# Moving modulation pieces between the stages of a weight stream, and a weight split ahead of the attention's quotients

## What is computed

```python
for l in range(DEPTH_2):
    mod = jax.nn.silu(c) @ w_ada[l] + b_ada[l]
    sh1, sc1, g1, sh2, sc2, g2 = jnp.split(mod[:, None, :], 6, axis=-1)
    h = x * (1.0 + sc1) + sh1
    y = token_mixer(h, ...)
    x = layer_norm_2(DEEPNORM_ALPHA * x + g1 * y, ln1_g[l], ln1_b[l])
    h = x * (1.0 + sc2) + sh2
    y = conv_ffn(h, ...)
    x = layer_norm_2(DEEPNORM_ALPHA * x + g2 * y, ln2_g[l], ln2_b[l])
```

## Time and profile before

| | |
|---|---|
| median of 3 runs | 1767.1 us |
| the profiled execution | 1769.27 us, span 1767.5 us |
| PE busy | 1724.4 us (98%) |
| DVE busy | 1488.2 us (84%) |
| ACT busy | 1101.6 us (62%) |
| POOL busy | 288.7 us (16%) |
| low halves on DVE | 469, 577.9 us |
| ada pieces on DVE | 96, 116.7 us |
| chain that ended last | PE 69%, DVE 15%, ACT 8% |

### The profile page before, as it was taken

How to read it: one execution, slowest core, us unless ns; L and a number is a source line. 1 busy time by engine, 2 the same in 40 slices (tenths; PEclk the granted TensorE clock), 3 DMA queues, 4 the chain that set the end, 5 groups by cost and what they waited for, 6 DMA issues and landing times.

```text
span 1767.5 us, 28648 instructions
## 1 busy us (share of the span) xinstructions
PE 1724.4 (98%) x10356; PEld 1508.1 (85%) x10356; DVE 1488.2 (84%) x2896; ACT 1101.6 (62%) x2180; POOL 288.7 (16%) x396
## 2 busy tenths in 40 slices
PE   9999999999999999999998999999999899999997
PEld 8888888888888888888887888888888888988886
DVE  6999879877799999699986888788787788789887
ACT  6888665554575555688863555576665456566664
POOL 3995000000000000298700000012000300002000
PEclk9999999999999999999998999999999999999999
DMA  7446658845558988344554744546764654546662
GB/s 246 149 150 191 194 179 287 264 164 189 199 195 289 318 293 298 122 148 137 188 177 155 238 144 144 197 126 203 225 197 150 212 196 129 174 140 190 224 184 80
DMA packets 92733, 339.48 MB, mean 192 GB/s; under 512 B 10288, under 2 KB 10672, under 8 KB 91952
## 3 DMA queue, kind: packets, MB, share of 16 engines
q1 hardware_dynamic: 92592, 337.64, 58.8%
HBM read 336.55 MB, written 1.05 MB: 191 GB/s over the span
## 4 chain that ended last, share of the span: by engine, by line
PE 69%; DVE 15%; ACT 8%; issue 4%; POOL 2%; DMA 1%; SPq 0%; ACTq 0%; DVEq 0%; POOLq 0%
PE ps L104 68%; DVE wl L120 6%; ACT tmp L110 3%; ACT wh L113 3%; POOL B L120 2%; PE ps L107 2%; DVE B L120 1%; DVE raw L130 1%; DVE tmp L130 1%; DVE tmp L120 1%; DMA cb<-in_cb 1%; DVE sm L142 1%; ACT B L110 1%; DVE sc L151 1%; ACT os L113 1%
## 5 line engine op out<-in xcount | busy, mean ns | idle before, releaser
L104 PE MATMUL ps<-XS,wh 128*128 128x256 f32 (+2 forms) x3152 | 782.0, 330 | 24.2 <-DVE wl L120 17.3
L120 DVE TENSOR_TENSOR wl<-raw,wh 128x1024 fp32r<-128x1024 f32 x469 | 577.9, 1246 | 93.6 <-ACT wh L113 91.5
L104 PEld LDWEIGHTS ps<-XS,wh 128*128 128x128 f32 (+1 forms) x3152 | 527.9, 193 | 81.0 <-issue 28.6
L104 PE MATMUL ps<-XS,wl 128*128 128x256 f32 x2136 | 581.3, 283 | 0.0
L113 ACT CAST wh<-raw 128x1024 fp32r<-128x1024 f32 x469 | 477.2, 1045 | 101.6 <-PE ps L104 94.6
L104 PEld LDWEIGHTS ps<-XS,wl 128*128 128x128 f32 x2136 | 409.6, 192 | 11.4
L120 POOL TENSOR_TENSOR B<-B,tmp 128x236 f32<-128x236 f32 (+11 forms) x368 | 244.2, 705 | 628.6 <-ACT tmp L110 612.7
L104 PE MATMUL ps<-wh,os 128*128 128x512 f32 x864 | 280.3, 392 | 0.9 <-DVE wl L120 0.5
L104 PE MATMUL ps<-B,raw 128*128 128x256 f32 x1024 | 226.1, 380 | 0.0
L130 DVE SCALAR_TENSOR_TENSOR ps<-B,C,ps 128x253 f32<-128x253 f32 (+17 forms) x560 | 216.7, 477 | 2.8 <-ACT ps L110 2.8
L104 PEld LDWEIGHTS ps<-B,raw 128*128 128x128 f32 x1024 | 192.6, 190 | 28.4 <-issue 2.9
(11 more groups left out here) (172 smaller groups left out, 1667.3 us busy)
## 6 DMA issues: line engine op xcount, KB each, us to landing
raw<-in_w SPq DMA_DIRECT2D x628, 512.0 KB, 4.4
B<-in_ln SPq DMA_DIRECT2D x4, 1024.0 KB, 6.0
C<-in_cst SPq DMA_DIRECT2D x1, 1103.5 KB, 9.2
X<-in_x SPq DMA_DIRECT2D x2, 512.0 KB, 4.6
out_x<-X SPq DMA_DIRECT2D x4, 256.0 KB, 2.5
cb<-in_cb SPq DMA_DIRECT2D x1, 512.0 KB, 13.7
pos<-in_pos SPq DMA_DIRECT2D x1, 160.0 KB, 5.5
raw<-in_w SPq DMA_DIRECT2D x1, 128.0 KB, 3.9
```

Of the source, the lines that this page charges most:

```text
L104: return NOTHING if self.e is None else self.e.matmul(*a, **k)
L120: return NOTHING if self.e is None else self.e.tensor_tensor(o, a, b, op)
```

## The change

The ada pieces keep their number and their order among themselves. The plan puts them elsewhere: 2 in a0 (after `o10` and `o11`), 45 in b, 26 in c, 1 in a1 (after `o10`), 7 in m0, 8 in f0 and 7 in m1. Among the heads there are now 26 instead of 12: one after each `b.z` from 2 on and one after each of `b.o2` to `b.o13`. In the token mixers none is left among `iq` and `qk`; three stand at `cq0`, `cq1` and `ckv` and four at the gate units `g8`, `g10`, `g12` and `g14`. In `dve_b`, `feed_dve("b.z{h}")` now stands ahead of `dve_quotients`. Two parts of the rotary work move: the first steps go ahead of a1's `z7`, and the spreading goes to m0, behind `feed_dve("m0.wr", 2)`.

```diff
-def plan_a(j):
+def plan_a(j, u):
...
     for k in range(16):
         out.append((f"{A}.o{k}", [("a_w_out", j, 128 * k, 128, 0, D)], "split"))
+        if k in ((10,) if j else (10, 11)):
+            out.append(ada_piece(j, next(u)))
     return out
...
@@ plan_b
-            if h > 1 and h % 2 or h in (4, 6, 10, 12, 14):
+            if h > 1:
                 out.append(ada_piece(0, next(u)))
         if h >= 2:
             out.append((f"b.o{h - 2}", [("b_w_out", 0, 128 * (h - 2), 128, 0, D)], "split"))
+            if 4 <= h < 16:
+                out.append(ada_piece(0, next(u)))
...
@@ plan_c
-            if i and (i < 14 or kind in "cu"):
+            if i and kind in "cu":
                 ada()
...
@@ plan_m
     for n in range(4):
         one(f"iq{n}", tiles(w, l, O_IQ + 128 * n))
-        if n < (3 if l else 4):
-            ada()
     for n in range(2):
         one(f"cq{n}", tiles(w, l, O_CQ + 128 * n))
+        ada()
     one("ckv", tiles(w, l, O_CKV))
+    ada()
     for n in range(8):
         one(f"qk{n}", tiles(w, l, 128 * n))
-        ada()
...
             one(f"g{n}", tiles(w, l, (O_GB if n < 8 else O_GA) + 128 * (n % 8)))
+            if n in (8, 10, 12, 14):
+                ada()
...
@@ plan_f
-            a = next(u, None) if i >= 18 else None
+            a = next(u, None) if 8 <= i < 16 else None
...
@@ dve_a
         self.feed_dve(dve, f"{A}.z6.1", 0)
+        if j:
+            self.dve_rope_turns(dve)
         self.feed_dve(dve, f"{A}.z7.0", 0)
...
             if j and i == 16:
                 self.dve_rope(dve)
-            if j and i == 18:
-                self.dve_rope_spread(dve)
...
@@ dve_b
+            h = st - 1
+            if 0 <= h < 16:
+                self.feed_dve(dve, f"b.z{h}")
             if st < 16:
                 self.dve_quotients(dve, self.tmp[st % 3], self.stat(st), ("b", st))
             if st == 1:
                 turned(10)
-            h = st - 1
-            if 0 <= h < 16:
-                self.feed_dve(dve, f"b.z{h}")
...
@@ dve_m
         self.feed_dve(dve, f"{M}.wr", 2)
+        if l == 0:
+            self.dve_rope_spread(dve)
```

More of the change, by code:

```diff
@@ L220, in plan_a, with plan_b @@
         out.append((f"{A}.o{k}", [("a_w_out", j, 128 * k, 128, 0, D)], "split"))
+        if k in ((10,) if j else (10, 11)):
+            out.append(ada_piece(j, next(u)))
     return out
-def plan_b():
+def plan_b(u):
     out = []
-    u = iter(range(48))
     def chunk(which, n, base, adas, kps=range(4)):
@@ L251, in plan_b @@
             out.append((f"b.o{h - 2}", [("b_w_out", 0, 128 * (h - 2), 128, 0, D)], "split"))
-    return out, u
+            if 4 <= h < 16:
+                out.append(ada_piece(0, next(u)))
+    return out
 def plan_c(u, u1):
@@ L370, in plan @@
 def plan():
-    b, u = plan_b()
-    u1 = iter(range(48))
-    out = plan_a(0) + b + plan_c(u, u1) + plan_a(1)
+    u, u1 = iter(range(48)), iter(range(48))
+    out = plan_a(0, u) + plan_b(u) + plan_c(u, u1) + plan_a(1, u1)
     u = u1
@@ L1358, in rope_views, with dve_rope_turns @@
         return [self.m["G"][64:96, k * T:k * T + T] for k in range(4)]
-    def dve_rope(self, dve):
+    def dve_rope_turns(self, dve):
         s, m, r = self.s, self.m, slice(64, 96)
@@ L1376, in dve_rope, with step @@
         dve.ts(k, k, -MAGIC, None, ALU.add, None).then_inc(s["rope"].up(3), 1)
+    def dve_rope(self, dve):
+        s = self.s
+        a, k, w, pf = self.rope_views()
+        def step(n):
+            dve.wait_ge(*s["rope"][n])
         step(3)
```

## The result

| | before | after |
|---|---|---|
| median of 10 runs | 1767.05 us | 1773.28 us |
| lowest to highest | 1765.9 to 1769.23 us | 1769.69 to 1774.7 us |
| profiled execution | 1769.27 us, span 1767.5 | 1769.69 us, span 1767.9 |

The ratio is 1.0032, 95% interval 1.0022 to 1.0042: slower by 6 us, where 16 were forecast. The two profiled executions differ by 0.4 us alone. Before's lies just above its ten runs, after's is the shortest of its ten; the other nine took 1772.2 to 1774.7 us, at a mean granted clock of 0.995 or 0.996 where the profiled one had 0.998. So I read the profile after as the change without the clock term; the first experiment tests that.

The account below looks back on a forecast made before the run. PE was taken as the bound, short of work in the mixing layers and hardly in the heads. Stage terms summed to +2.4 us, the clock added +13.2: 1767.1 + 15.6 = 1783 us, range 1765 to 1795.

Parts of the forecast that it names:

- the clock term: Heads and a0: half-speed stretches behind eleven new PE waits, taken at 1.2 us each, +13.2 us.
- Heads: Ten rounds of heads: a loop through DVE, PE and ACT makes each round 10.10 us, PE waiting 2.5: +22.9 us.
- Rival 3: Heads: the loop doesn't close, as o{st-3}'s cast is done before head st's maxima end; 1752 us, chance 0.08.
- a0, a1, m0's entry, f0: Stages outside heads and mixing layers: a0 +3.1, a1 +0.2, m0's entry -1.0, f0 +1.5 us.
- m0 and m1: Mixing layers: PE's waits behind ada pieces mostly go and the clock recovers; m0 -9.9, m1 -14.4 us.
- The mean clock over the ten rounds: Heads, a sign of the forecast: mean granted clock near 0.85, half of 3.35 us lost in each 11.3.
- Rival 2: Heads: PE waits 2.5 us a head but the clock holds its upper level; 1769.5 us, chance 0.18.

Follow-up runs that it names:

- the first experiment: The changed kernel once more, without an edit, to profile another execution: 1775.87 us.
- the longer waits above: The changed kernel with a useless DVE maximum ahead of the low halves of o3 to o12: 1797.05 us with 1024 columns, 1781.66 us with 256.

## Why the prediction was too high

- **Heads.** Right in mechanism and size: 10.08 us a round against 10.10, a wait of 2.24 to 2.5. The stage lost 25.5 instead of 22.9, as the first of the waits is 3.5 us, the low half of `b.z5` is late by 0.6 as well, and another 0.9 comes behind the tenth round. Rival 3 is excluded by the rows: the cast stands behind the exponentials.
- **a0, a1, m0's entry, f0.** 3.6 against 3.1, 0.1 to 0.4 against 0.2, -1.0 against -1.0, 1.6 against 1.5.
- **m0 and m1.** Too small a gain: -13.2 against -9.9 and -16.1 against -14.4. Two things were left out. DVE's backlog from the ada pieces had reached as far as the gate units `g0` and `g1`, where PE waited too (about 1 us a unit in either layer, gone now). And the half-speed stretch at m0's entry, which was to stay, is gone (1.4 us), though the wait ahead of it is 1.4 us still. In the kernel before it stands here:

```profile
940.90:944.10 3.20, 3.20 (x16) 3.20 (x16) 1.64 (x4) 1.71 (x6) 0.00 (x0) 0.50 0.00 0
```

- **The clock in the heads and a0: the step that failed.** It took 1.2 us for each of eleven waits, 13.2; in the median run the term is about 3.6 by my estimate, which is what that run has beyond the profiled execution. A stretch costs more than that where it comes (1.5, and 2.7 where it is double), but it doesn't come behind each: none of eleven in one profile, three in another. The mean clock over the ten rounds, forecast near 0.85, was 1.00 in the one and 0.95 in the other. Without the clock term the sum is +2.4. The two profiled executions, of which the second has no such stretch, differ by +0.4; the median after lies 3.6 above its profiled execution, and the median before 2.2 below, which makes the 6.2. That +2.4 came so near to +0.4 is in part luck: b and a0 lost 3.1 more than forecast, and m0 and m1 gave 5.0 more. The reason that was given, that the waits of the mixing layers were of this size and had 0.50 beside them, took length for the cause; the longer waits above show that it isn't by itself.
- **Rival 2** came nearest: 1769.5 with the clock held. It was given 0.18, and the row that spoke for it (1.00 throughout the heads) was discounted, since its waits were short. The median lies between it and the forecast, nearer to it.

By the section "HAM oscillation — how this bites in real kernels" of the Trainium skill's "TensorE: Matmul & The Clock Gate", which warns only of longer idle gaps than a0's and nine of the ten in the heads, that rival would have been the forecast. The runs agree with it in part: in the profile after no wait had 0.50 behind it, the first of 3.5 us included, and in the next profile eight of the ten in the heads had none. But the wait of 2.8 us at a0 had 0.50 behind it in seven of nine profiles.

## What to carry to other kernels

Ahead of moving work between stages, follow the loop of the stage that receives it through every engine: here the 30 us that the mixing layers and m0's entry gave were paid out again in b, a0 and f0, most of it because a lookahead counts pieces, and one piece more put a weight into the round that uses it. A call that is moved ahead of another gains only if what it waits for is ready by then; here its cast was released by the same chain, one step later. And a cost that may or may not come, taken eleven times over, belongs in the range and not in the middle of the forecast, until a row shows it in that place.

## What the runs showed of the hardware

Waits of PE of the same length were followed by a stretch at 0.50 or not, within one execution (2.56 us: six in a row not, then two and one of 2.72) and between executions of the same kernel (the change: none, then three). Where it came, a stretch lasted about 3.4 us, or twice that, and cost 1.4 to 1.6 us, or 2.5 to 2.9. So one execution's granted clock is a sample: ten runs of the changed kernel spread over 5 us, with the same order of work. What decides whether a stretch comes stays open.
